# ScalarE takes VectorE's PSUM copies in the parameter stage of a hybrid layer, with a third place for modulation weights

## The reference, cut to what matters

```python
mod = jax.nn.silu(c) @ w_ada + b_ada                     # 1024 -> 6 * 1024, for prompt and sample
sh1, sc1, g1, sh2, sc2, g2 = jnp.split(mod[:, None, :], 6, axis=-1)
...
dt = jnp.exp(log_dt)[:, None]                            # 32 groups, 64 states each
decay = jnp.exp(ar * dt)
lam_re, lam_im = decay * jnp.cos(ai * dt), decay * jnp.sin(ai * dt)
coef_re = ((lam_re - 1.0) * ar + lam_im * ai) / den
coef_im = (lam_im * ar - (lam_re - 1.0) * ai) / den
bb_re = coef_re[..., None] * br - coef_im[..., None] * bi
bb_im = coef_re[..., None] * bi + coef_im[..., None] * br
...
y = einsum(c_re, h_re) - einsum(c_im, h_im) + d_skip * u  # h: scan over positions with lam
```

## Time and profile before

| | before |
|---|---|
| median of 3 runs | 1643.91 us (1643.09 to 1644.66) |
| the profiled execution | 1641.81 us, its span 1639.7 us |
| TensorE, VectorE, ScalarE, GpSimd busy | 86%, 48%, 27%, 11% of the span |
| the stage `ssm_parameters` | 265.9 to 380.6 us, 114.7 us |
| its VectorE chain | 265.97 to 380.60 us |

### The profile page before, as it was taken

One profiled execution on the slowest core, in us unless ns is written; L12 is line 12 of the kernel. 1 busy time (PEld: TensorE's weight loads), 2 busy tenths in 40 slices (PEclk: granted clock), 3 DMA queues, 4 the chain that ended last, 5 costly groups with the idle time before them and its releaser, 6 DMA issues. The chain is left out here.

```text
span 1639.7 us, 20173 instructions
## 1 busy us (share of the span) xinstructions
PE 1408.3 (86%) x7245; PEld 805.6 (49%) x7246; DVE 781.2 (48%) x1688; ACT 449.5 (27%) x969; POOL 186.1 (11%) x377
## 2 busy tenths in 40 slices
PE   6799997776889999999959998989982799999970
PEld 1455553555644456666636665644442344444430
DVE  0412224967628778889955564433345121212117
ACT  3311112111235547667134554001120111111110
POOL 0000004003001011122110000000000222222220
PEclk9899998897978999999989999999995799999995
DMA  9300005753022152241040000532327666875828
GB/s 335 139 5 4 4 4 146 227 182 50 6 47 57 37 176 95 67 133 53 28 188 2 1 2 32 203 101 103 116 88 247 225 216 229 286 271 200 287 78 325
DMA packets 137992, 204.77 MB, mean 125 GB/s; under 512 B 27557, under 2 KB 103013, under 8 KB 137573
## 3 DMA queue, kind: packets, MB, share of 16 engines
q1 hardware_dynamic: 122642, 160.13, 29.9%
q0 software_dynamic: 10656, 32.49, 5.5%
q10 hardware_dynamic: 4612, 11.05, 1.9%
HBM read 158.71 MB, written 42.93 MB: 123 GB/s over the span
## 5 line engine op out<-in xcount | busy, mean ns | idle before, releaser
L2143 PE MATMUL ps<-ex_wgu,ex_xT 128*128 x416 | 185.3, 599 | 3.9 <-DVE ex_xT L2209 2.7
L1300 DVE TENSOR_SCALAR_CACHE_REDUCE tk_eq<-sc,tk_cand 128x512 bf16<-128x512 f32 (+4 forms) x155 | 146.8, 1007 | 0.0
L1698 PE MATMUL ps<-hT,mergedT 128*128 128x512 f32 (+1 forms) x288 | 120.3, 601 | 4.8 <-DMA op_wr<-in_w_route_expert 4.8
L2143 PEld LDWEIGHTS ps<-ex_wgu,ex_xT 128*128 128x128 f32 x416 | 77.8, 192 | 93.3 <-issue 93.3
L1234 PE MATMUL ps<-zT,gt_w 128*128 128x352 f32 (+1 forms) x384 | 120.9, 468 | 0.0
L1234 PE MATMUL ps<-hT,gt_w 128*128 128x352 f32 (+1 forms) x336 | 105.8, 468 | 0.0
L2216 DVE SCALAR_TENSOR_TENSOR ex_hid<-ex_silu,ex_weight,ps 128x256 f32<-128x256 f32 x26 | 12.5, 480 | 184.8 <-ACT ex_silu L2188 184.8
L1234 PEld LDWEIGHTS ps<-zT,gt_w 128*128 128x128 f32 x384 | 73.0, 190 | 44.1
L2164 PE MATMUL ps<-ex_wd,ex_hidT 128*128 x208 | 93.6, 593 | 0.2 <-DVE ex_hidT L2223 0.2
L1263 ACT ACTIVATE mask<-sc,tk_cand 128x384 bf16<-128x384 f32 (+1 forms) x62 | 82.3, 1330 | 14.7 <-DVE tk_cand L1316 14.7
L1698 PEld LDWEIGHTS ps<-hT,mergedT 128*128 128x128 f32 (+1 forms) x288 | 50.9, 186 | 68.5 <-issue 63.0
(11 more groups left out here) (468 smaller groups left out, 2181.7 us busy)
## 6 DMA issues: line engine op xcount, KB each, us to landing
ex_wgu<-in_w_gate SPq DMA_DIRECT2D x16, 1024.0 KB, 5.4
ex_wgu<-in_w_up SPq DMA_DIRECT2D x16, 1024.0 KB, 8.0
ex_wd<-in_w_down SPq DMA_DIRECT2D x16, 1024.0 KB, 5.2
sp_ada_w<-in_w_ada SPq DMA_DIRECT2D x14, 1024.0 KB
cb_y<-y_dram ACTq DMA_DIRECT2D x16, 512.0 KB, 6.9
merge_left_dram<-qiT SPq DMA_DIRECT2D x8, 544.0 KB, 6.2
mg_gb<-gate_b_dram SPq DMA_DIRECT2D x8, 544.0 KB, 3.9
mergedT<-merge_left_dram SPq DMA_DIRECT2D x8, 544.0 KB, 4.8
```

Source lines behind the costliest of these rows:

```text
L1300: return v.tensor_scalar(junk[j], m.sc[0:r, c:c + w], scalar, 0.0, op, ALU.add, accum_out=cnt[0:r, j:j + 1])
L1698: i = nc.tensor.matmul(m.ps[rows, 2 * (t % 2) + n, :], m.mergedT[:, k, t * P:t * P + r], m.wout[:, k, n * 512:(n + 1) * 512], start=k == 0 ...
L2143: j = nc.tensor.matmul(m.ps[:, 2 + b, :], xT[:, b, k, :], wgu[:, bass.ds(at, 1), k, :].rearrange("p o n -> p (o n)"), start=k == 0, stop=k ...
```

## The change

ScalarE instead of VectorE copies the input matrices (`copy_w`) and the kernel rows (`copy_k`) from PSUM. The modulation weights get a third place in the lower half of `m.M`; ScalarE's queue loads the first three chunks, and `m.M` is cleared in two halves, the lower one after the last chunk. Each part of C is loaded by 4 transfers of 128 partitions instead of 16 of 16 partitions. On TensorE the chunks are spread differently: 3 + 3 beside the first six spans, chunk 6 between the two groups of input matrices, 7 to 9 beside the last spans, 10 to 15 between and behind the quarters of the kernel rows. VectorE goes from the products of C straight to the rotation table.

```diff
+    KERNEL_CHUNKS = ((10,), (11,), (12, 13), (14, 15))
...
-        aw = sb("sp_ada_w", [P, 2, KD, AC])
+        two = sb("sp_ada_w", [P, 2, KD, AC])
+        aw = [two[:, 0], two[:, 1], m.M[:, 0:G // 2, :].rearrange("p g n -> p (g n)").rearrange("p (k n) -> p k n", k=KD)]
...
         def load_c(engine, j):
             a = (A.ssm_c_re, A.ssm_c_im)[j]
-            for q in range(PAIR):
-                dst = cin[J * (q % 8):J * (q % 8 + 1), j, q // 8, :].rearrange("j (g p) -> j g p", g=2)
-                engine.dma_start(dst, a[2 * q:2 * q + 2].rearrange("g j p -> j g p")).then_inc(lc if j == 0 else lc1, 16)
+            for h in range(2):
+                for g in range(2):
+                    engine.dma_start(cin[:, j, h, ST * g:ST * (g + 1)],
+                                     a[16 * h + g:16 * h + 16:2]).then_inc(lc if j == 0 else lc1, 16)
...
-                for i in range(2, len(ada)):
-                    sp.wait_ge(aps, i - 1)
+                for i in range(3, len(ada)):
+                    sp.wait_ge(aps, i - 2)
                     load_mod_weights(sp, i)
-                    if i == 2:
+                    if i == 4:
                         gates.load(sp, 2)
...
-                nc.gpsimd.memset(m.M[:, :, :], 0.0).then_inc(mz, 1)
+                nc.gpsimd.memset(m.M[:, G // 2:, :], 0.0)
                 for s in range(len(gates.spans)):
                     gates.store(pool, s)
+                pool.wait_ge(aps, len(ada))
+                nc.gpsimd.memset(m.M[:, 0:G // 2, :], 0.0).then_inc(mz, 1)
                 gates.all_stored(pool)
...
-                filler(range(0, 3), range(0, 4))
+                filler(range(0, 3), range(0, 3))
...
-                filler(range(3, 6), range(4, 8))
+                filler(range(3, 6), range(3, 6))
                 pe.wait_ge(wtr, 1)
                 input_matrices(range(0, 6))
-                filler(range(6, 9), range(8, 12))
+                filler((), range(6, 7))
+                input_matrices(range(6, 8))
+                filler(range(6, 9), range(7, 10))
+                pe.wait_ge(wev, 8)
                 pe.wait_ge(bbr, 1)
-                input_matrices(range(6, 8))
-                pe.wait_ge(wev, 8)
...
-                    if x == 2:
-                        filler((), range(12, len(ada)))
+                    filler((), KERNEL_CHUNKS[x])
...
+                def copy_w(x):
+                    act.wait_ge(wps, x + 1)
+                    nc.scalar.copy(m.W[:, x // 4, 4 * (x % 4):4 * (x % 4) + 4, :].rearrange("p q n -> p (q n)"),
+                                   m.ps[:, x % 6, :]).then_inc(wev, 1)
+
+                def copy_k(x):
+                    act.wait_ge(kps, x // 2 + 1)
+                    g0 = 8 * (x // 2) + x % 2
+                    nc.scalar.copy(ksb[:, g0:min(g0 + 8, G):2, :],
+                                   m.ps[0:J, x % 6, :].rearrange("j (g n) -> j g n", n=P)).then_inc(kcp, 1)
...
-                load_mod_weights(nc.scalar, 0)
-                load_mod_weights(nc.scalar, 1)
+                for i in range(3):
+                    load_mod_weights(nc.scalar, i)
...
-                filled(range(0, 3), range(0, 4))
-                filled(range(3, 6), range(4, 8))
-                filled(range(6, 9), range(8, 12))
-                filled((), range(12, len(ada)))
+                filled(range(0, 3), range(0, 3))
+                filled(range(3, 6), range(3, 6))
+                for x in range(6):
+                    copy_w(x)
+                filled((), range(6, 7))
+                for x in range(6, 8):
+                    copy_w(x)
+                filled(range(6, 9), range(7, 10))
+                for x in range(4):
+                    copy_k(2 * x)
+                    copy_k(2 * x + 1)
+                    filled((), KERNEL_CHUNKS[x])
...
-                for x in range(8):
-                    dve.wait_ge(wps, x + 1)
-                    v.tensor_copy(m.W[:, x // 4, 4 * (x % 4):4 * (x % 4) + 4, :].rearrange("p q n -> p (q n)"),
-                                  m.ps[:, x % 6, :]).then_inc(wev, 1)
...
-                for x in range(8):
-                    dve.wait_ge(kps, x // 2 + 1)
-                    g0 = 8 * (x // 2) + x % 2
-                    v.tensor_copy(ksb[:, g0:min(g0 + 8, G):2, :],
-                                  m.ps[0:J, x % 6, :].rearrange("j (g n) -> j g n", n=P)).then_inc(kcp, 1)
```

More of the change, by code:

```diff
@@ L444, in ssm_parameters @@
         a1, a2, a3, th, trig = m.sem("sp_dt"), m.sem("sp_decays"), m.sem("sp_adt"), m.sem("sp_angles"), m.sem("sp_trig")
-        aw = sb("sp_ada_w", [P, 2, KD, AC])
-        ab = m.vs[DEC:DEC + 1, 0:8, :].rearrange("o b d -> o (b d)").rearrange("o (a n) -> o a n", a=2)
+        two = sb("sp_ada_w", [P, 2, KD, AC])
+        aw = [two[:, 0], two[:, 1], m.M[:, 0:G // 2, :].rearrange("p g n -> p (g n)").rearrange("p (k n) -> p k n", k=KD)]
+        ab = m.vs[DEC:DEC + 1, 0:12, :].rearrange("o b d -> o (b d)").rearrange("o (a n) -> o a n", a=3)
         arow = m.vs[32:34, 0:8, :].rearrange("s b d -> s (b d)").rearrange("s (a n) -> s a n", a=2)
@@ L450, in ssm_parameters @@
                           "sp", m.ga_loaded)
-        awl = [m.sem(f"sp_ada_w_loaded{i}") for i in range(2)]
+        awl = [m.sem(f"sp_ada_w_loaded{i}") for i in range(3)]
         kcp, cte, lc1 = m.sem("sp_k_copied"), m.sem("sp_cT_copied"), m.sem("sp_c_im_loaded")
@@ L461, in load_c @@
             a = (A.ssm_c_re, A.ssm_c_im)[j]
-            for q in range(PAIR):
-                dst = cin[J * (q % 8):J * (q % 8 + 1), j, q // 8, :].rearrange("j (g p) -> j g p", g=2)
-                engine.dma_start(dst, a[2 * q:2 * q + 2].rearrange("g j p -> j g p")).then_inc(lc if j == 0 else lc1, 16)
+            for h in range(2):
+                for g in range(2):
+                    engine.dma_start(cin[:, j, h, ST * g:ST * (g + 1)],
+                                     a[16 * h + g:16 * h + 16:2]).then_inc(lc if j == 0 else lc1, 16)
         def load_mod_weights(engine, i):
             j = ada[i]
-            engine.dma_start(aw[:, i % 2, :, :], wada[:, :, j * AC:(j + 1) * AC]).then_inc(awl[i % 2], 16)
-            engine.dma_start(ab[:, i % 2, :], A.b_ada[:, j * AC:(j + 1) * AC]).then_inc(awl[i % 2], 16)
+            engine.dma_start(aw[i % 3], wada[:, :, j * AC:(j + 1) * AC]).then_inc(awl[i % 3], 16)
+            engine.dma_start(ab[:, i % 3, :], A.b_ada[:, j * AC:(j + 1) * AC]).then_inc(awl[i % 3], 16)
         with nc.Block() as block:
@@ L497, in mod_chunk @@
                 def mod_chunk(i):
-                    pe.wait_ge(awl[i % 2], 32 * (i // 2 + 1))
+                    pe.wait_ge(awl[i % 3], 32 * (i // 3 + 1))
                     if i:
@@ L503, in mod_chunk @@
                             nc.tensor.matmul(m.ps[32 * x:32 * x + 2, 7, 0:AC // 4], m.cT[:, k, :],
-                                             aw[:, i % 2, k, AC // 4 * x:AC // 4 * (x + 1)], start=k == 0, stop=False)
+                                             aw[i % 3][:, k, AC // 4 * x:AC // 4 * (x + 1)], start=k == 0, stop=False)
                     for x in range(4):
                         j = nc.tensor.matmul(m.ps[32 * x:32 * x + 2, 7, 0:AC // 4], m.ones[DEC:DEC + 1, 0:2],
-                                             ab[:, i % 2, AC // 4 * x:AC // 4 * (x + 1)], start=False, stop=True)
+                                             ab[:, i % 3, AC // 4 * x:AC // 4 * (x + 1)], start=False, stop=True)
                     j.then_inc(aps, 1)
@@ L530, in _ @@
                 nc.tensor.transpose(m.ps[:, 0, 0:DEC + PAIR], m.sp_rows[:, 0:P], m.ident[0:DEC + PAIR, 0:DEC + PAIR]).then_inc(tr, 1)
-                filler(range(0, 3), range(0, 4))
-                pe.wait_ge(lc, 16 * (3 + PAIR))
-                pe.wait_ge(lc1, 16 * PAIR)
+                filler(range(0, 3), range(0, 3))
+                pe.wait_ge(lc, 16 * 7)
+                pe.wait_ge(lc1, 16 * 4)
                 for j in range(4):
@@ L650, in _ @@
                 step(v.tensor_tensor(ci, ci, rden, ALU.mult))
-                dve.wait_ge(lc, 16 * (3 + PAIR))
+                dve.wait_ge(lc, 16 * 7)
                 tv = tmp[:, 0:PAIR * J].rearrange("p (q j) -> p q j", j=J)
```

## The result

The changed kernel took **1630.0 us** in the median (1628.76 to 1633.34, 4 runs), the kernel before beside it 1644.29 (1643.09 to 1648.9, 4 runs): a ratio of 0.9918 [0.9903, 0.9933], 14.3 us less. I had forecast 1620.6. The direction held, the size did not: the time lies above my own range (1618 to 1625.5) and on the upper end of the one that takes in the first two rivals (1616.5 to 1630).

The account below looks back on a forecast made before the run. TensorE and VectorE waiting for each other bound the parameter stage. Its end moves from 380.6 to 357.3, 23.3 us less: 1641.81 to 1618.5 profiled, 1620.6 median; own range 1618 to 1625.5, with the first two rivals 1616.5 to 1630.

Parts of the forecast that it names:

- the first two rivals: Queue takes the third pair freely and VectorE bounds the end (1617.4, chance 0.15); last weights bound the end (1626.8, chance 0.12).
- ScalarE's queue is held: Front of the parameter stage: the third pair of weight loads delays table load, Exp, Sin and span 1 by 4.2 us.
- The early MEMSET half meets nothing: GpSimd's early zeroing, 1.8 us, falls while VectorE waits for Exp; 2.27 us saved.
- VectorE is then 1.6 us ahead of before: VectorE at C in the parameter stage: it arrives at 287.3 instead of 288.94, so products of C end at 329.3.
- Four quarters of kernel rows and six chunks: 7.2 + 7.3; twice a chunk follows a chunk and waits 1.06: TensorE's tail at the end of the parameter stage, from 337.1 to 353.7.
- that the stretch behind the stage keeps its length: Behind the parameter stage: everything moves earlier with the stage's end, so the 23.3 us comes off the whole time.
- the last of the prediction's own signs of being wrong: Prediction is wrong if the stretch behind the parameter stage changes its own length by over 3 us.
- The queue that takes the third pair freely: Rival, stage front: third pair costs 1.2 us instead of 4.2, VectorE bounds the end; gain 26.4, 1617.4 us; chance 0.15.
- the queue held for 17.5 us: Rival, stage front: ScalarE's queue is held as SyncE's was; gain 10.0, 1633.9 us; chance 0.10.
- the returning waits: Rival, kernel rows: ScalarE's copies, queued behind modulation rows, end where VectorE's ended; 1643.9 us; chance 0.03.
- the low clock for good: Rival, TensorE after span 1's wait: the clock stays low, costing 49 us against 23.3; 1669.6 us; chance 0.04.
- the rival in which the last weights bound the end: Stage end: each of the last four weight loads needs 5.4 us alone; gain 17.1, 1626.8 us; chance 0.12.

Follow-up runs that it names:

- v1: Changed kernel with the sixteen copies of input matrices and kernel rows back on VectorE: 1645.8 us, ratio 1.0017 to the kernel before.
- o1: Changed kernel with TensorE's order of before, ScalarE copying in that order: 1632.23 us, ratio 0.9931 to the kernel before.
- e1: Changed kernel with ScalarE's first gate copy and first modulation row ahead of Sin: 1625.67 us, ratio 0.9887 to the kernel before.
- a1: The changed kernel run again, unaltered: 1629.7 us, ratio 0.9907 to the kernel before.
- a3: Changed kernel with the second and third places of the weights swapped, so chunks 11 and 14 read the ordinary tile: 1628.81 us, one run.
- b1: The changed kernel once more, unaltered, five rounds: 1627.42 us, ratio 0.9906 to the kernel before.
- s1: Changed kernel with 32 small matmuls (64 trace records) added on TensorE ahead of gate span 0: 1627.39 us, one run.
- a4: Changed kernel with chunks 10 to 15 in two groups of 128 columns instead of four of 64: 1623.13 us, one run.
- a2: Changed kernel with the third pair of weights loaded by SyncE's queue, behind C: 1626.58 us, ratio 0.9898 to the kernel before.
- p2: Changed kernel with C in 16 and 16 transfers again: 1632.56 us, ratio 0.9928 to the kernel before.

## Why the prediction was right and where it was wrong

*Right.* The stage is TensorE's and VectorE's waits for each other, and ScalarE's copies take them away (v1, and o1 for the old order). ScalarE's queue is held for 4.3 us (4.2 forecast), the table load comes at 8.4 into the stage. The kernel rows start at 71.6 (71.2). C is not waited for. The early MEMSET half meets nothing. No chunk after the first waits for weights, so the last weights do not bound the end, and VectorE's end is hidden.

*Wrong, at no cost here:* "VectorE is then 1.6 us ahead of before", with the products of C done at 329.3. They ended 66.9 us into the stage, 3.5 later than that: VectorE must wait for span 2, because `wt` lies where that span's weights lie (`dve.wait_ge(gates.psum, 3)`), and spans 1 and 2 had moved with ScalarE's copy. The wait was in the code and I did not follow it. It cost the forecast nothing, as TensorE came to the kernel rows later than VectorE, but it was a trap: e1 shows that the front had 3.3 us to give. The wait ahead of span 1 cost 1.5 us of low clock on top (6.51 against 5.00; 1.1 forecast).

*Wrong: "Four quarters of kernel rows and six chunks: 7.2 + 7.3; twice a chunk follows a chunk and waits 1.06".* This term was 16.6 us and measured 23.4 (340.58 to 363.96). The gaps inside chunks 11 and 14 are 1.30 + 2.65 = 3.95 of the 6.8 missing. The low clock after the second gap is about 1.7: chunk 15 took 0.9 more than at full clock, the rest of chunk 14 about 0.8 (1.66 and 0.39 for 53 of 64 records and the bias, where 0.9 and 0.29 would do). The four quarters took 1.94 each instead of 1.81, 0.5. Some 0.6 are spread over the rest. I summed durations as if TensorE could always be fed; the chunk's price came from a stretch with 5 us spans in between. Shown are three things: the gaps keep their place in the stream of instructions (a1, a3, b1), move with it (s1, the second one), and go with half the instructions (a4).

The seventeen traces tie them to the packets of 16 KB as well. Count TensorE's matmul records from the start of the stage: all 24 gaps of over 0.3 us with the label "issue" stand ahead of record 1074, 1201, 1202 or 1329, which is 127 or 128 records from one place to the next, and each ends 1.2 to 1.5 us after the end of a packet. Where one of these places has no gap, the last packet had ended 1.2 to 6.8 us before TensorE came to it (2.17 in s1, record 1074). This fits a TensorE that stands until a packet has come. That the packets hold its instructions is a reading too: the trace's word for them is "instruction", and what is in them no view shows. Why a packet comes in time or late was not tested and stays open.

The sign was in the trace before. Chunk 14 is a row of 43 records, and the rest of it follows in another row, behind a gap with the same label, ahead of record 1329 there too:

```profile
363.88 0.81 PE L503 MATMUL ps<-sp_ada_w,cT 128*2 128x64 f32 x21 [0.41 <-issue]
```

I read the wait of 3.17 us ahead of the first row and passed over the "x43".

*Wrong: that the stretch behind the stage keeps its length.* In the profile on record the stage gave 16.05 us, the stretch ahead of it took 3.07 more (268.99 against 265.92), and what lies behind it 4.6 more, of which 2.5 in the scan stage; so 8.4 us came there, and 14.3 between the medians. With 4.6 the last of the prediction's own signs of being wrong, over 3 us behind the stage, was met. The scan stage took 101.2 to 109.4 us in seventeen profiles, with code that none of the kernels altered, and 107.4 to 109.3 in three of the changed kernel. Stretches of the kernel before, 40 to 70 us behind the stage's end (columns as in the earlier trace rows):

```profile
420.90:430.90 10.00, 7.68 (x56) 6.16 (x54) 9.55 (x14) 2.59 (x4) 0.56 (x1) 0.83 0.05 19
430.90:440.90 10.00, 8.72 (x113) 6.04 (x112) 0.84 (x4) 3.45 (x7) 0.00 (x0) 1.00 0.01 2
440.90:450.90 10.00, 7.68 (x46) 5.88 (x48) 9.58 (x13) 2.14 (x3) 0.00 (x0) 0.83 0.00 0
```

and of the changed kernel:

```profile
407.90:417.90 10.00, 7.68 (x54) 6.27 (x52) 9.57 (x13) 2.59 (x4) 0.57 (x1) 0.76 0.05 18
417.90:427.90 10.00, 8.94 (x80) 5.10 (x78) 0.25 (x2) 3.28 (x7) 0.00 (x0) 0.73 0.01 2
427.90:437.90 10.00, 7.46 (x66) 5.93 (x68) 7.32 (x10) 2.31 (x5) 0.00 (x0) 0.96 0.00 1
```

The granted clock (the number behind the engines) is low in other places: 0.73 in a stretch that had 1.00. What sets this is open; no run tested it, and whether the change itself lengthens the scan stage by some us or not stays open with it. The stretch ahead of the stage, which no kernel altered either, took 264.8 to 269.0 us in the same profiles. So a few us of scatter lie on either side of the stage, and the forecast had no term for them.

*The rivals.* The queue that takes the third pair freely (4.29 us held), the queue held for 17.5 us, the returning waits and the low clock for good did not come. The measured 1630.0 lies near the sum of the rival in which the last weights bound the end (1626.8), but by another mechanism.

## What to carry to other kernels

Where a change packs hundreds of small instructions of one engine into a few microseconds, a sum of their durations can be too short, here by 3.95 us of gaps: search the trace for a group that is cut in the middle with "issue" as its releaser, and give the new dense stretch a gap or two. Follow each wait that stands behind a moved instruction across engines, also those that only guard a reused buffer. And take each part back alone, but measure the steps between as well: here the copies were worth 17.5 us beside the new order and 8.9 beside the old one, and the third place nothing.

## What the runs showed that I had not expected

- TensorE stood up to 2.65 us inside a run of independent matmuls with all operands there, at one of a few places that are fixed in its instruction stream: 255 records lie between the two gaps of the changed kernel (28 + 8 of chunk 11, 32, 72 and 72, 32, and 11 of chunk 14). In the changed kernel's first profile the matmuls behind the gap of 2.65 ran at the low clock (1.66 for 53 records, then 1.89 for 64); behind the gap of 1.30 they did not. In a1 the 53 records behind 2.65 took 0.95.
- A VectorE operation that takes 0.17 us was held for 3.33 (a2) and 3.60 (p2). Both ended with GpSimd's MEMSET, but began 1.5 and 1.7 us ahead of it, while GpSimd still issued its transfers.
- Half the matmuls with twice the columns were slower: 2.16 us for a chunk in two groups, 1.22 in four (a4).
